# Two more buffers for split expert weights, in the place of x and two used gates, in the first expert layer

## What is computed

```
    cap = EC_CAPACITY_FACTOR * t // N_EXPERTS
    aff = jax.nn.softmax(jnp.einsum('btd,de->bte', h, w_router).astype(jnp.float32), axis=-1)
    gates, idx = lax.top_k(jnp.swapaxes(aff, 1, 2), cap)
    xs = jax.vmap(lambda hb, ib: hb[ib])(h, idx)
    a = jnp.einsum('becd,edf->becf', xs, w_gate)
    ...
```

## Time and profile before

| | us |
|---|---|
| median of three runs (2776.39 to 2781.73) | 2777.67 |
| the profiled execution | 2793.83 |
| its span, first to last instruction | 2792.5 |
| first matmul on a piece (line 1852) | 1081.1 |
| end of the last one | 1730.1 |
| PE busy in the span | 2387.6 (85%) |
| DVE busy | 1342.0 (48%) |
| ACT busy | 985.3 (35%) |

### The profile page before, as it was taken

The page is one execution under the profiler, slowest core; times in us unless marked ns, Lnnn a source line. Parts: engine busy times, 40 slices in busy tenths (PEclk is TensorE's granted clock), DMA queues, the critical chain, the costliest instruction groups (busy, mean ns, idle before and its releaser), DMA issues.

```text
span 2792.5 us, 26448 instructions
## 1 busy us (share of the span) xinstructions
PE 2387.6 (85%) x10239; PEld 1369.7 (49%) x10239; DVE 1342.0 (48%) x2548; ACT 985.3 (35%) x1620; POOL 203.8 (7%) x268
## 2 busy tenths in 40 slices
PE   4998988999899966999899997679999868777786
PEld 2444543456586433666666665346677423222222
DVE  2147425437764045888788875366674141111111
ACT  2024233115543024777777774344442000000000
POOL 0000000001100100011101110000000100000000
PEclk8999898999999977999999999889999979999999
DMA  6122501110000086899899988200001489999998
GB/s 251 60 87 94 181 1 64 61 45 31 1 1 2 31 322 219 323 341 325 330 337 346 328 330 295 105 1 1 1 1 62 148 340 402 403 402 401 399 408 346
DMA packets 92346, 546.30 MB, mean 196 GB/s; under 512 B 7711, under 2 KB 10543, under 8 KB 67518
## 3 DMA queue, kind: packets, MB, share of 16 engines
q1 hardware_dynamic: 81806, 518.95, 48.1%
q0 software_dynamic: 6144, 20.98, 3.1%
q10 hardware_dynamic: 4272, 4.69, 0.5%
HBM read 523.62 MB, written 20.97 MB: 195 GB/s over the span
## 4 chain that ended last, share of the span: by engine, by line
PE 55%; DMA 22%; DVE 11%; ACT 8%; issue 4%; ACTq 0%; POOL 0%; SPq 0%; DVEq 0%; POOLq 0%
DMA AR<-in_w_exp_gate_dram 13%; PE PS L1852 8%; PE PS L1478 7%; PE PS L631 6%; PE PS L654 6%; PE PS L798 5%; PE PS L2022 4%; DMA AR<-in_w_exp_up_dram 4%; PE PS L642 3%; ACT AR L1913 3%; PE PS L1185 2%; DVE RW L1818 2%; ACT RW L1810 2%; PE PS L1019 2%; DMA AR<-in_w_exp_down_dram 2%
## 5 line engine op out<-in xcount | busy, mean ns | idle before, releaser
L1818 DVE TENSOR_TENSOR RW<-AR,RW 128x2048 fp32r<-128x2048 f32 x192 | 435.3, 2287 | 91.5 <-ACT RW L1810 91.1
L2022 PE MATMUL PS<-AR 128*64 128x512 f32 x1536 | 373.8, 634 | 99.5 <-DMA AR<-in_w_exp_gate_dram 47.9
L1810 ACT CAST RW<-AR 128x2048 fp32r<-128x2048 f32 x192 | 363.3, 1907 | 211.3 <-PE PS L1852 128.2
L1852 PE MATMUL PS<-RW,RX 128*96 128x512 f32 x1536 | 385.9, 411 | 54.9 <-DVE RW L1818 43.2
L1852 PEld LDWEIGHTS PS<-RW,RX 128*96 128x96 f32 x1536 | 258.0, 170 | 173.7 <-DVE RW L1818 51.7
L2022 PEld LDWEIGHTS PS<-AR 128*64 128x64 f32 x1536 | 114.4, 144 | 334.0 <-issue 264.3
L631 PE MATMUL PS<-AR 128*128 128x256 f32 (+5 forms) x640 | 239.8, 493 | 6.9 <-ACT AR L674 3.8
L654 PE MATMUL PS<-AR 128*128 128x128 f32 x1600 | 212.2, 280 | 5.8 <-DVE AR L756 4.3
L674 ACT ACTIVATE AR<-PS,AR 128x768 f32<-128x768 f32 (+1 forms) x160 | 130.5, 816 | 219.3 <-DVE AR L724 134.4
L654 PEld LDWEIGHTS PS<-AR 128*128 128x128 f32 x1600 | 196.3, 196 | 17.1 <-issue 15.7
L1478 PE MATMUL PS<-AR 128*128 128x512 f32 (+1 forms) x480 | 194.3, 562 | 3.2 <-DMA AR<-in_w_in_even_dram 3.2
(11 more groups left out here) (320 smaller groups left out, 2432.4 us busy)
## 6 DMA issues: line engine op xcount, KB each, us to landing
AR<-in_w_exp_gate_dram SPq DMA_DIRECT2D x64, 2048.0 KB, 12.4
AR<-in_w_exp_up_dram SPq DMA_DIRECT2D x64, 2048.0 KB, 27.9
AR<-in_w_exp_down_dram SPq DMA_DIRECT2D x64, 2048.0 KB, 13.0
AR<-in_w_ada_dram SPq DMA_DIRECT2D x30, 2048.0 KB, 8.5
AR<-in_w_in_dram SPq DMA_DIRECT2D x6, 2048.0 KB, 7.7
AR<-in_w_in_even_dram SPq DMA_DIRECT2D x4, 2048.0 KB, 8.2
AR<-in_w_out_dram SPq DMA_DIRECT2D x2, 2048.0 KB, 8.3
AR<-in_w_out_even_dram SPq DMA_DIRECT2D x2, 2048.0 KB, 7.8
```

Source lines behind the costliest of these rows:

```text
L1810: s.copy(pair(i)[0], raw_half(key, hf)).then_inc(*S.up("hi", l, i))
L1818: v.tensor_tensor(lo, raw_half(key, hf), hi.bitcast(F32), ALU.subtract).then_inc(*V.up("split", key, hf))
L1852: m = pe.matmul(bank(ob)[0:Mc, :], st_, mv[:, k, 512 * q_:512 * q_ + 512], start=(k0 + k == 0 and n_ == 0), stop=(k0 + k == 7 and n_ == 2))
L2022: m = pe.matmul(bank(b)[64 * q_:64 * q_ + 64, :], op, w[:, c, 512 * q_:512 * q_ + 512], start=(h == 0 and c == 0), stop=(h == 1 and c == 3 ...
```

## The change

It adds two buffers `RW3` and `RW4` of 16 KB a partition at addresses 0 to 32 KB, which hold x (0 to 16 KB), the context (16 to 24 KB) and the gates `GB[0]` and `GB[1]` (24 to 32 KB). All of these have been used by then; x and the context lie in HBM once `x_rows` is written. Piece i now lies in `RW[i % 5]`, ACT waits for the use of piece i-5, and the lists of ACT and DVE run five pieces ahead. The first pieces of the two new buffers wait for `xw` and for the last read before the stage.

```
-        ctx.enter_context(nc.sbuf_tensor("gap0", [128, 87 * 256], F32))
+        RWX = [ctx.enter_context(nc.sbuf_tensor(f"RW{i}", [128, 4096], FR)) for i in (3, 4)]
+        ctx.enter_context(nc.sbuf_tensor("gap0", [128, 55 * 256], F32))
...
-        RW = [ctx.enter_context(nc.sbuf_tensor(f"RW{i}", [128, 4096], FR)) for i in range(3)]
+        RW = [ctx.enter_context(nc.sbuf_tensor(f"RW{i}", [128, 4096], FR)) for i in range(3)] + RWX
...
         def pair(i):
-            return RW[i % 3][:, 0:2048], RW[i % 3][:, 2048:4096]
+            return RW[i % 5][:, 0:2048], RW[i % 5][:, 2048:4096]
...
             if i < 3:
-                if l:
-                    S.wait_ge("used", 0, len(PIECES[0]) - 3 + i)
                 S.wait_ge("full", MLAST[l], 1, OUTP[MLAST[l]] - 1)
+            elif i < 5:
+                S.wait_ge("xw", l)
+                S.wait_ge("read", MLAST[l], 1, OUTP[MLAST[l]] - 1)
             else:
-                S.wait_ge("used", l, i - 3)
+                S.wait_ge("used", l, i - 5)
...
-            for nsp in range(3):
+            for nsp in range(5):
                 act_split(l, nsp)
...
-            for nsp in range(3):
+            for nsp in range(5):
                 dve_split(l, nsp)
```

## The result

| | before | after |
|---|---|---|
| median of 4 runs, us | 2779.70 | 2806.78 |
| ratio, 95% interval | | 1.0097 [1.0077, 1.0117] |
| profiled execution, span, us | 2793.8, 2792.5 | 2807.63, 2806.3 |
| period of an expert, 13 of them, us | 40.07 | 42.07 |
| first to last matmul on a piece, us | 649.0 | 670.5 |

The change made the kernel **slower, by 27.1 us**. The forecast was 47 us faster, and 2806.8 lies outside the range. The last two rows of the table hold the whole loss: 21.5 + 5.7 = 27.2 us.

The account below looks back on a forecast made before the run. It took PE and ACT to be short of split buffers, with DMA next at 36.8 us a period. Terms -42.5 + 3.8 - 5 - 3 = -46.7 us against the 2777.7 median gave 2731 us, range 2711 to 2760.

Parts of the forecast that it names:

- 13 periods: Thirteen expert periods between turn_x bursts: each falls from 40.07 to 36.8 us, 42.5 us less in all.
- the start: Two more casts stand ahead of the first turn_x's activations, delaying PE's first matmul: +3.8 us, up to +4.7.
- the first experts: Before the 13 periods, one stall of the same kind, with its slow clock, is saved: -5 us.
- the end: After the 13 periods, one stall of 2.8 us with its slow clock is saved: -3 us.
- The casts ahead of turn_x: With five buffers PE needs the piece at 14.9 us and has it at 11.5, so its stall goes.
- Everything else: PE's, POOL's and SP's lists stay; DVE and ACT do as much as before, covered by idle time: no cost.
- rival E: Slower: at turn_a, products and casts stand behind splits of a late load, +25 us, 2803 us; chance 0.05.
- The hole at turn_x: DMA's 3.6 us hole at each turn_x closes because PE no longer pauses; 0.4 us left for it.
- Rival D: All of DMA's hole at turn_x stays, raw buffers set a 40.0 us period: 2777 us; chance 0.04.
- B: Half of DMA's hole at turn_x stays, 38.5 us a period: 2753 us; chance 0.21.
- C: PE decides, loads run as in the second layer, 35.4 us a period: 2713 us; chance 0.15.
- What would show it: Signs expected in the profile after, among them period 36 to 37.6 us, DMA share 0.97 or more, PE's clock 1.00.

Follow-up runs that it names:

- run 1: The changed kernel with the gather of expert e+3 issued ahead of the scatter of expert e; 2774.31 us, ratio 0.9981.
- run 2: The changed kernel with each place's other operations on ACT and DVE ahead of the second of its two splits; 2875.70 us, ratio 1.0361.
- run 4: The kernel before, with three split buffers, and only the gather of expert e+3 put ahead of the scatter of e; 2776.44 us, ratio 0.9998.
- run 9: The changed kernel with a one-input TENSOR_REDUCE of about the same length in place of DVE's subtraction; 2782.92 us, ratio 1.0007.
- run 3: The changed kernel with both the gather ahead of the scatter and the other operations ahead of the second split; 2748.06 us, ratio 0.9890.
- Run 12: The kernel of run 8 with the operations behind both splits again and the start of the change; 2745.57 us, ratio 0.9884.
- run 8: The kernel of run 7 with four split and four raw buffers in place of five and three; 2732.34 us, ratio 0.9843.
- run 7: The kernel of run 3 with the splits of pieces 3 and 4 moved behind the first turn_x; 2740.64 us, ratio 0.9878.
- run 5: The changed kernel with a one-input scalar multiplication by 0 in place of DVE's subtraction; 2758.07 us, ratio 0.9942.

## Why the prediction was wrong

By its own terms, in us; "measured" compares lengths in the two traces:

| term | forecast | measured |
|---|---|---|
| 13 periods | -42.5 | +26.0 |
| the start | +3.8 | +5.7 |
| the first experts | -5 | -1.8 |
| the end | -3 | -2.8 |
| sum | -46.7 | +27.1 |

The last two are 50.6 against 48.9 us from the first matmul to the first of the 13 periods, and 77.4 against 74.6 from the last to the stage's end.

*The casts ahead of turn_x: right.* PE's wait for split pieces fell from 38.5 us to none, as the count of 14.9 against 11.5 said.

*"Everything else": the step that failed.* It let the new rhythm of DVE cost nothing, since "their idle time covers it". DVE's load was counted as time on DVE alone. The gaps between its subtractions had another use: POOL's scatter finished in them. With the subtractions beside the scatter back to back, POOL's part went from 3.3 us on average to 9.0, and the gather behind it, whose turn_x had waited for nothing, came up to 9.5 us late (runs 1, 2, 4 and 9). The hint stood in the trace of before: one and the same POOL instruction took 1.4, 2.7 or 4.9 us. The prediction used neither those rows nor the slack of the gather; it says that PE's, POOL's and SP's lists stay, and a list that stays does not keep its times. This step is worth about 31.5 us (run 1). The rest of the missing saving stood at turn_a, at rival E's place: with the order mended as well, the time falls by another 26 us (run 3).

*Rival E: the right place and the wrong price.* It named turn_a and line 1875, and 2803 us, close to the 2806.8 measured, at a chance of 0.05. The closeness is partly luck. It asked for a load that is late by two pieces in 15 experts and for DMA to have got slower. Run 12 shows the wait with every load in time. In the change it cost 25.0 us in 13 periods, in eight of the 13 experts, and the larger part came from the gather, which no rival named.

*The hole at turn_x: wrong as to its cure.* I let it close because PE no longer paused. With both causes removed (run 3) DMA reaches 0.95 and 37.98 us, and ACT waits for loads. It took the fourth raw buffer to reach 0.98. The 36.4 us of DMA's work a period were about right: run 8 has a period of 36.58 with DMA busy for 0.98 of it, 35.8 us. It is also 44.8 us faster than before, nearly the 46.7 forecast, but by way of four things that the change did not have: the gather ahead, the operations ahead, the mended start and a fourth raw buffer in the place of the fifth split buffer. So it does not bear out the forecast of 36.8 for the change.

*Rival D's time.* By the terms that B and C use, -0.9 - 4.2, it would be 2773 us and not 2777; its sum left out the end. Nothing else hangs on it.

*The start: the right sign, and short by 1.9 us.* The third load was expected to have landed 10.5 to 12.2 us after its issue; it took 13.2:

```profile
1054.00 7.80 SPq L2615 DMA_DIRECT2D AR<-in_w_exp_up_dram  x2
...
1067.25 1.90 ACT L1812 CAST RW<-AR 128x2048 fp32r<-128x2048 f32 x1 [2.95 <-DMA AR<-in_w_exp_up_dram]
1069.05 4.61 ACT L1915 ACTIVATE AR<-PS,AR 128x64 f32<-128x64 f32 x16
...
1075.84 6.45 PE L1854 MATMUL PS<-RW,RX 128*96 128x512 f32 x20 [17.47 <-DVE RX L1953]
```

*What would show it.* "PE's clock at 1.00 through the stage" and "DMA 0.97 or more" both failed (0.93 and 0.88), and the sign given for E, a wait at line 1875, appeared, in eight of the 13 experts. The list had no sign for POOL.

## What to carry to other kernels

Where more buffers close the gaps between one engine's instructions, ask who used the gaps: list the instructions of the other engines whose length varies in the trace of before, and look at what overlapped the long ones. Put a transfer that someone waits for ahead of one that nobody does in the same queue; here that was worth nothing with three buffers and 31 us with five. A deeper look-ahead in a list written out by hand also moves every other operation of that list back, so move the operations and the buffers together, and divide the room between the stages of the pipeline rather than give it all to the one that stalls.

## What the runs showed of the hardware

- POOL's part of a scatter takes 1.4 us alone. Beside DVE's TENSOR_TENSOR with both inputs in SBUF (128x2048 f32, 2.29 us) it took up to 14.94 us, and up to 20.27 in runs 2, 3 and 7; beside a TENSOR_REDUCE of the same length, 1.45. The Trainium skill ("SBUF — State Buffer", Who interferes with whom) says that a DVE instruction with two SBUF inputs contends with a GpSimd instruction that reads SBUF, and that tensor_reduce on trn2 never contends. The trace agrees with both, as far as these instructions go. In the same place it infers that tensor_tensor does not hold up the writing of descriptors; the scatters of the change were held up, and whether by the reading of the index list or by something else no run here shows.
- One scatter began in the first of six subtractions, with no gap between them but two products of DVE, and outlasted them all. How POOL gets its turn between two DVE instructions, and why it does so sometimes after one and sometimes after six, stays open.
- With DVE's operation at 1.23 us and one input (run 5) the scatters took at most 1.98 us.
- Run 8 moved 364 GB/s over 13 periods with stores and loads mixed, at a DMA share of 0.98.
